# Sliding-window attention's q and k turned by VectorE through DRAM instead of by TensorE

## The chip, the cores and the metric

One core of a Trainium2 chip runs the whole program. The metric is the device time of one execution in microseconds (us); for the kernel before, three executions took 1803.64, 1803.77 and 1804.32, median 1803.77.

## What is computed

Two layers of a decoder trunk over 512 tokens of width 2048, float32 in and out. Per layer: RMS norm, one input projection (2048 x 7192), four mixers of four heads each, side by side, each times a SiLU gate, and one output projection (2048 x 2048) plus the residual. The mixers are called A (gated linear attention, GLA), B (sliding window attention), C (differential attention) and D (gated delta net). B and C matter here:

```
# B: 4 query heads and 2 key heads of 128, window of 128 tokens, tile N of 128 queries sees tiles N-1 and N
q = rms_norm(q.reshape(Bn, N, W, G, R, d), q_g);  k = rms_norm(k.reshape(Bn, N, W, G, d), k_g)
s = jnp.einsum('bgrnid,bgnjd->bgrnij', q, kb) * d ** -0.5
s = jnp.where(valid, s - m_h * dist, -jnp.inf)
mx = jnp.maximum(jnp.max(s, -1), sink); p = exp(s - mx); p = p / (sum(p) + exp(sink - mx))
o = jnp.einsum('bgrnij,bgnjd->bgrnid', p, vb)
# C: 4 heads with two q and two k of 64 each
q = rms_norm(q.reshape(Bn, T, H, 2, dq), q_g) * dq ** -0.5;  k = rms_norm(k.reshape(Bn, T, H, 2, dq), k_g)
w = softmax(s[0]) - lam_full * softmax(s[1]);  o = w @ v
```

## The kernel before

The order of each engine is written out by hand, as five instruction streams with semaphores. `Steps` (line 67) numbers the steps of one stream on one semaphore; `X.one("3.q")` marks the step, `X.at(l, "3.q")` is the value that others wait for. Letters: B_PE, B_ACT, B_DVE are B's steps on TensorE, ScalarE and VectorE, N_ACT and N_DVE those of the norms of B's and C's q and k.

TensorE works through dense products (`project`, line 539): one of 14 chunks of 512 columns of the input projection, 16 steps of the inner dimension (kt) times 4 banks times 3 matmuls, then the output projection. Weights stream in through the SP and POOL queues. Between these dense matmuls `project` opens breaks: it takes `stages` pieces from a generator (`mixer`), spread evenly over half steps of 6 dense matmuls each, starting after `skip` steps. A piece ends at a `yield`. TensorE executes in order, so when a piece waits for an operand, the dense product behind it waits too. Each chunk's four banks (`acc`) are taken out by ScalarE (`take_out`, line 1052), and the next chunk's first matmul in a bank waits for that.

The order of chunks is dq dk dv dz bz az aq av bq bkv cq ck cv cz. GLA's tiles 0 to 3 are spread over bq, bkv, cq and ck. B's tiles 0 and 1 are spread over cv, its tiles 2 and 3 over cz (line 1018, 13 pieces each). C follows during the output projection.

A tile t of B in the kernel before, on TensorE (`swa`, line 772): values of tile t-1 and, in the same break, six transposes of the tile's normed q (4 heads) and k (2 heads) (L796, L798); in the next break the scores (L808); three breaks later the turned weights (L824); two later the next tile's values (L783). The two-digit names in the code (`s0`, `s1`, `pt0`, `pt1`) are two heads each. ScalarE copies the turned q and k out of PSUM with their gains (L1382, L1384), and takes the exponentials (L1397). VectorE adds the slopes (L1988), makes maxima, copies half of the turned weights (L2009, step PT1) and scales the outputs (L2020).

C's q and k are turned already without TensorE: squares on ScalarE (L1344), sums (L1948) and products with the inverse norms (L1961) on VectorE, then VectorE transposes of 32 x 32 blocks (L1975), four DMAs from ScalarE's queue into the DRAM tensor `hops` (L1393) and eight back (`hop_back`, L1364), which put the blocks in their places. All four tiles must be back when C starts, long after. For B and C the norms of tile t+1 are made during tile t: `squares`, `sums`, `inverses` (logarithm and exponential, each with a table load) and `normalise`, q and k of both mixers together.

DMAs that ScalarE issues stand in its instruction order. In the trace they are on ACTq.

## Time and profile before

| | |
|---|---|
| median of three executions | 1803.77 us |
| the profiled execution | 1804.25 us, its span 1802.5 us |
| granted TensorE clock, mean over the span | 1.000 |
| PE busy | 1795.4 us |
| VectorE, ScalarE, GpSimd busy | 917.9, 501.3, 920.8 us |
| local attention of layer 0 (cv and cz) | about 589 to 692 us |

The profile is of one execution. A timeline row gives start, length, engine, line, operation, the written and the read tensor, the shape and the count of merged instructions; in square brackets stands how long the engine was idle before and what it waited for. Matmuls are pipelined, so their lengths overlap; the distance of two starts says more. Lines are those of the kernel before.

### The profile page before, as it was taken

To read this page: it belongs to the slowest core of one execution; us is meant where nothing else is said; L and a number is where in the kernel's file an instruction comes from. 1 tells how busy PE (TensorE), PEld (TensorE's weight loads), DVE (VectorE), ACT (ScalarE), POOL (GpSimd) and SP (SyncE) were. 2 spreads that over 40 slices of the span, in tenths; PEclk is the share of its full clock that TensorE was granted. 3 is DMA by queue.
4 is the path that set the end of the run, shared out by engine and by line. 5 is a ranking of instruction groups with operands and counts; after the bars stand their busy time and mean duration, and the time that the engine had idled before them with its cause. 6 is when DMAs were issued, how large, how long until landed. Compare 5 with 4: busy or idle time off the path is not lost.

```text
span 1802.5 us, 23457 instructions
## 1 busy us (share of the span) xinstructions
PE 1795.4 (100%) x9254; PEld 1478.6 (82%) x9254; DVE 917.9 (51%) x1959; ACT 501.3 (28%) x959; POOL 920.8 (51%) x864
## 2 busy tenths in 40 slices
PE   9999999999999999999999999999999999999999
PEld 7788888888888888788887888888888888887887
DVE  7546825525433675544644478264344337755342
ACT  6212214022222543322312131141222225333220
POOL 6555544545555444445565555445455555444444
PEclk9999999999999999999999999999999999999999
DMA  7566554655555667455775656545555566674556
GB/s 276 166 189 210 168 161 152 183 149 177 182 177 175 207 199 251 140 160 175 253 225 171 188 187 192 159 149 180 158 175 181 165 186 200 201 254 140 164 164 210
DMA packets 108334, 333.39 MB, mean 185 GB/s; under 512 B 11680, under 2 KB 24512, under 8 KB 107968
## 3 DMA queue, kind: packets, MB, share of 16 engines
q1 hardware_dynamic: 43904, 155.73, 27.3%
q0 software_dynamic: 40320, 146.82, 26.8%
q10 hardware_dynamic: 24000, 29.34, 4.8%
q8 instruction: 73, 1.20, 0.3%
q14 instruction: 37, 0.30, 0.1%
HBM read 319.25 MB, written 12.60 MB: 184 GB/s over the span
## 4 chain that ended last, share of the span: by engine, by line
PE 95%; DVE 3%; DMA 1%; ACT 1%; issue 0%; SPq 0%; ACTq 0%
PE acc L563 84%; PE mix L612 2%; PE mix L853 1%; DVE actT_lo L1536 1%; DMA w_raw<-in_wstream 1%; PE mix L783 1%; PE mix L873 1%; PE mix L808 1%; PE mix L606 1%; PE mix L886 1%; DVE slots L2028 0%; PE mix L760 0%; PE mix L982 0%; PE mix L963 0%; DVE slots L1564 0%; DMA slots<-in_x 0%
## 5 line engine op out<-in xcount | busy, mean ns | idle before, releaser
L520 POOL TENSOR_TENSOR w_lo<-w_raw,w_hi 128x512 fp32r<-128x512 f32 x575 | 761.2, 1326 | 616.6 <-DMA w_hi<-in_wstream 462.7
L563 PE MATMUL acc<-w_hi,actT_hi 128*128 128x512 f32 x1408 | 558.8, 397 | 0.0
L563 PE MATMUL acc<-w_hi,actT_lo 128*128 128x512 f32 x1408 | 548.7, 390 | 0.0
L563 PE MATMUL acc<-w_lo,actT_hi 128*128 128x512 f32 x1408 | 548.4, 389 | 0.0
L563 PE MATMUL acc<-actT_hi,w_hi 128*128 128x512 f32 x896 | 357.5, 399 | 0.8 <-issue 0.4
L563 PE MATMUL acc<-actT_hi,w_lo 128*128 128x512 f32 x896 | 349.5, 390 | 0.0
L563 PE MATMUL acc<-actT_lo,w_hi 128*128 128x512 f32 x896 | 349.3, 390 | 0.0
L563 PEld LDWEIGHTS acc<-w_hi,actT_hi 128*128 128x128 f32 x1408 | 264.5, 188 | 55.5 <-issue 2.8
L563 PEld LDWEIGHTS acc<-w_hi,actT_lo 128*128 128x128 f32 x1408 | 264.3, 188 | 55.7
L563 PEld LDWEIGHTS acc<-w_lo,actT_hi 128*128 128x128 f32 x1408 | 264.6, 188 | 51.9
L491 POOL DMA_DIRECT2D w_hi<-in_wstream x280 | 159.2, 569 | 252.6 <-PE acc L563 239.3
L563 PEld LDWEIGHTS acc<-actT_hi,w_hi 128*128 128x128 f32 x896 | 168.3, 188 | 47.1 <-issue 12.8
L563 PEld LDWEIGHTS acc<-actT_hi,w_lo 128*128 128x128 f32 x896 | 168.2, 188 | 35.9
L563 PEld LDWEIGHTS acc<-actT_lo,w_hi 128*128 128x128 f32 x896 | 168.5, 188 | 32.9 <-issue 0.5
L2028 DVE TENSOR_TENSOR slots<-acc,slots 128x512 f32<-128x512 f32 x64 | 42.8, 689 | 84.8 <-PE acc L563 84.8
L1626 DVE SCALAR_TENSOR_TENSOR slots<-slots,pcol_all 128x511 f32<-128x511 f32 (+2 forms) x72 | 84.7, 1181 | 1.7
L1058 ACT ACTIVATE slots<-acc,xr 128x512 f32<-128x512 f32 x56 | 37.8, 690 | 167.9 <-PE acc L563 167.9
L1606 DVE TENSOR_TENSOR slots<-acc,slots 128x512 f32<-128x512 f32 x24 | 15.7, 688 | 125.0 <-PE acc L563 91.8
L1882 DVE SCALAR_TENSOR_TENSOR slots<-mix,slots 128x256 f32<-128x256 f32 x8 | 3.4, 424 | 133.3 <-ACT slots L1301 133.3
L612 PEld LDWEIGHTS mix<-slots 128*128 128x128 f32 x400 | 48.5, 191 | 2.0
L612 PE MATMUL mix<-slots 128*128 128x128 f32 x400 | 49.0, 275 | 0.0
L1874 DVE STREAM_TRANSPOSE slots<-slots 32x512 f32<-32x512 f32 x64 | 45.0, 703 | 1.9
(269 smaller groups left out, 1608.3 us busy)
## 6 DMA issues: line engine op xcount, KB each, us to landing
w_raw<-in_wstream SPq DMA_DIRECT2D x288, 512.0 KB, 4.5
w_hi<-in_wstream POOLq DMA_DIRECT2D x280, 512.0 KB, 3.8
out_x<-slots ACTq DMA_DIRECT2D x7, 1024.0 KB, 8.4
slots<-hops ACTq DMA_DIRECT2D x64, 64.0 KB, 2.7
slots<-in_x ACTq DMA_DIRECT2D x1, 4096.0 KB, 19.4
slots<-out_x ACTq DMA_DIRECT2D x1, 4096.0 KB, 19.9
slots<-in_x SPq DMA_DIRECT2D x3, 1024.0 KB, 12.5
slots<-rows ACTq DMA_DIRECT2D x2, 1024.0 KB, 7.3
```

Of the source, the lines that this page charges most:

```text
L491: pool.dma_start(w_hi[:, g % HI].rearrange("p a n -> p (a n)"), wstream[g:g + 1].rearrange("a p n -> p (a n)")).then_inc(hi_in[g % HI], 16)
L520: pool.tensor_tensor(w_lo[:, n % RING], w_raw[:, g % RAW, k], w_hi[:, g % HI, k].bitcast(F32), ALU.subtract).then_inc(w_ready, 1)
L563: last = nc.tensor.matmul(acc[b][:, :], lhsT, rhs, start=(k == 0 and i == 0), stop=(k == kts - 1 and i == 2))
L606: last = nc.tensor.transpose(mh[i][:, h], s[:, h, t * P:t * P + P], ident)
L612: last = nc.tensor.matmul(mh[bank][:, h], lhsT[:, h], rhs[:, h], start=True, stop=True)
L783: last = nc.tensor.matmul(mh[2][:, h], W["PT"][:, h, P * m:P * m + P], kv[:, t + 1 - n + m, 256 + (h // 2) * HD:256 + (h // 2) * HD + HD], ...
L808: last = nc.tensor.matmul(mix[2 + h // 2][:, 256 * (h % 2):256 * (h % 2) + P * n], W["QT"][:, h], kv[:, t + 1 - n:t + 1, (h // 2) * HD:(h ...
L853: last = nc.tensor.matmul(mix[m][:, 0:P * n], qT[r, t, h], kT[r, 0:n, :, h].rearrange("p t b c -> p (t b) c"), start=True, stop=True)
L1058: nc.scalar.activation(slot(SLOT[c])[:, b], acc[b][:, :], ACT.Copy, scale=r) \
L1626: dve.scalar_tensor_tensor(dst[:, d:], src[:, 0:SEQ - d], tap[i], dst[:, d:], ALU.mult, ALU.add).then_inc(CONV_DVE.sem, CONV_DVE.one(f"{c} ...
L1874: dve.transpose(dst[fs, :, :, rs_], src[rs_, :, :, fs]) \
L2028: dve.tensor_tensor(xs, acc[b][:, :], xs, ALU.add).then_inc(acc_free, 1)
```

## The change

1. B's q and k are turned like C's: VectorE transposes of 32 x 32 blocks in one instruction each (q 512 columns, k 256), two stores per tile into a new DRAM tensor `hops_b`, eight loads back (`b_out`, `b_back`), all from ScalarE's queue. q returns to its slot, is copied with both gains into QT (the gain of k is multiplied into that of q at the start); k returns to its slot and is read there by the scores.
2. TensorE's transposes go. The scores of tile t stand in the break of the values of tile t-1, one break earlier than before; the scores of a pair of tiles are two matmuls of 128 columns per head instead of one of 256. The scores use banks 0 and 1, the turned weights 2 and 3 (it was the other way round).
3. The norms are split in two streams: B's two tiles ahead, C's one tile ahead. B's tiles 0 and 1 are normed within GLA's last tile, and tile 0 is turned and stored there.
4. C's turns are one instruction each for q and k; the source buffers are `general` (which its squares use too), two stores of 256 KB instead of four of 128 KB. C's q comes back into `ws` and is scaled from there into its slot (`scaled_q`), tile by tile.

Core of the diff, old helpers that only move left out:

```diff
-        out += ([f"{t-1}.pv"] if t else []) + [f"{t}.{x}" for x in "tr s0 s1 pt0 pt1".split()]
+        out += ([f"{t-1}.pv"] if t else []) + [f"{t}.{x}" for x in "s0 s1 pt0 pt1".split()]
...
-SWA_ACT = "gate qT kT p0 p1 p2 p3 es PT0".split()
+SWA_ACT = "gate qT p0 p1 p2 p3 es PT0".split()
 SWA_DVE = "b0 b1 b2 b3 mx mxs nm es g3 den rd PT1 y0 y1 y2 y3".split()
-TURNED = "q0 q1 k0 k1".split()
-
-NORM_ACT = "bq bk cq ck lnb lnc rb rc".split()
-NORM_DVE = "redb redc bq bk cq ck".split()
+TURNED = "q k".split()
+
+NORM_B_ACT, NORM_B_DVE = "q k ln r".split(), "red q k".split()
+NORM_C_ACT, NORM_C_DVE = "q k ln r".split(), "red q k".split()
...
-        turned_piece = dict(q0=smT[:, 0:256], q1=smT[:, 256:512], k0=wlr_sb[:, :], k1=s6[:, 768:1024])
+        turned_b = dict(q=smT[:, :], k=wlr_sb[:, :])
+        turned_c = dict(q=general[:, 0], k=general[:, 1])
...
-                pe.wait_ge(N_DVE.sem, N_DVE.at(l, f"{t}.bk"))
-                for h in H:
-                    nc.tensor.transpose(mh[0][:, h], q[:, t, h * HD:h * HD + HD], ident)
-                for g in range(2):
-                    last = nc.tensor.transpose(mh[1][:, g], kv[:, t, g * HD:g * HD + HD], ident)
-                last.then_inc(B_PE.sem, B_PE.one(f"{t}.tr"))
-                yield
-
-                pe.wait_ge(B_ACT.sem, B_ACT.at(l, f"{t}.kT"))
-                if t:
-
-                    pe.wait_ge(B_DVE.sem, B_DVE.at(l, f"{t-1}.y3"))
+                pe.wait_ge(hop_b_k, 64 * (TILES * l + t + 1))
+                pe.wait_ge(B_ACT.sem, B_ACT.at(l, f"{t}.qT"))
                 n = min(t, 1) + 1
                 for h in H:
-                    last = nc.tensor.matmul(mix[2 + h // 2][:, 256 * (h % 2):256 * (h % 2) + P * n], W["QT"][:, h],
-                                            kv[:, t + 1 - n:t + 1, (h // 2) * HD:(h // 2) * HD + HD],
-                                            start=True, stop=True)
+                    for m in range(n):
+                        c = 256 * (h % 2) + P * m
+                        last = nc.tensor.matmul(mix[h // 2][:, c:c + P], W["QT"][:, h], kT[:, t + 1 - n + m, h // 2],
+                                                start=True, stop=True)
                     if h % 2:
...
-                pe.wait_ge(B_ACT.sem, B_ACT.at(l, f"{t}.kT"))
+                if t:
+                    pe.wait_ge(B_DVE.sem, B_DVE.at(l, f"{t-1}.y3"))
                 for i in range(2):
 
                     pe.wait_ge(B_ACT.sem, B_ACT.at(l, f"{t}.p{2*i+1}"))
                     for h in (2 * i, 2 * i + 1):
                         for m in range(n):
-                            last = nc.tensor.transpose(mix[i][:, 256 * (h % 2) + P * m:256 * (h % 2) + P * m + P],
+                            last = nc.tensor.transpose(mix[2 + i][:, 256 * (h % 2) + P * m:256 * (h % 2) + P * m + P],
                                                        W["SB"][:, h, P * m:P * m + P], ident)
                     last.then_inc(B_PE.sem, B_PE.one(f"{t}.pt{i}"))
                 yield
                 yield
+                yield
...
+                def b_out(t):
+
+                    for c, cs in (("q", slice(0, GW)), ("k", slice(GW, GW + 256))):
+                        act.wait_ge(TB_DVE.sem, TB_DVE.at(l, f"{t}.{c}"))
+                        act.dma_start(hops_b[l, :, t, cs], turned_b[c]).then_inc(hop_b_out, 16)
+
+                def b_back(t):
+
+                    act.wait_ge(hop_b_out, 32 * (TILES * l + t + 1))
+                    for to, start, n, landed in ((slot(SLOT["bq"])[:, t], 0, P, hop_b_q),
+                                                 (slot(SLOT["bkv"])[:, t, 0:256], GW, 2 * BLK, hop_b_k)):
+                        for r in range(P // BLK):
+                            act.dma_start(to[BLK * r:BLK * r + BLK].rearrange("p (b c) -> p b c", b=P // BLK),
+                                          hops_b[l, :, t, start + n * r:start + n * r + n]
+                                          .rearrange("(b p) c -> p b c", b=P // BLK)).then_inc(landed, 16)
...
+                    if t == TILES - 1:
+                        act.wait_ge(acc_free, acc_free_after(l, CHUNKS.index("bkv"), 3))
+                        w(A_DVE, "ki")
+                        for i in range(2):
+                            squares_b(i)
+                            inverses(i, None)
...
+                    if t == TILES - 1:
+                        b_out(0)
...
+                def scaled_q(t):
+
+                    act.wait_ge(hop_q, 64 * (TILES * l + t + 1))
+                    nc.scalar.activation(slot(SLOT["cq"])[:, t].rearrange("p (h b c) -> p h b c", h=HEADS, c=BLK),
+                                         ws[:, :].rearrange("p (b h c) -> p h b c", h=HEADS, c=BLK), ACT.Copy,
+                                         scale=pcv(l, PC["gq_c"])).then_inc(Q_ACT.sem, Q_ACT.one(f"q{t}"))
+
+                def c_out(t):
+
+                    for i, c in enumerate("qk"):
+                        act.wait_ge(TC_DVE.sem, TC_DVE.at(l, f"{t}.{c}"))
+                        act.dma_start(hops[l, i, :, t], turned_c[c]).then_inc(hop_out, 16)
+
+                b_back(0)
                 act.wait_ge(acc_free, acc_free_after(l, CHUNKS.index("ck"), 3))
                 act.wait_ge(A_DVE.sem, A_DVE.at(l, f"{TILES-1}.y3"))
-                squares(0)
-                inverses(0)
+                squares_c(0)
+                inverses(None, 0)
                 for t in T:
                     w = lambda st, s, t=t: act.wait_ge(st.sem, st.at(l, f"{t}.{s}"))
                     s = lambda step, t=t: (B_ACT.sem, B_ACT.one(f"{t}.{step}"))
-                    kv = slot(SLOT["bkv"])[:, t]
                     if t:
 
                         act.wait_ge(B_DVE.sem, B_DVE.at(l, f"{t-1}.g3"))
                     nc.scalar.activation(W["GATE"], slot(SLOT["bz"])[:, t].rearrange("p (h c) -> p h c", h=HEADS),
                                          ACT.Tanh).then_inc(*s("gate"))
-                    w(B_PE, "tr")
-                    nc.scalar.activation(W["QT"], mh[0], ACT.Copy, scale=pcv(l, PC["gq_b"])) \
-                        .then_inc(*s("qT"))
-                    nc.scalar.activation(kv[:, 0:256], mix[1][:, 0:256], ACT.Copy,
-                                         scale=pcv(l, PC["gk_b"])).then_inc(*s("kT"))
+                    act.wait_ge(hop_b_q, 64 * (TILES * l + t + 1))
+                    nc.scalar.activation(W["QT"].rearrange("p h (b c) -> p h b c", c=BLK),
+                                         slot(SLOT["bq"])[:, t].rearrange("p (b h c) -> p h b c", h=HEADS, c=BLK),
+                                         ACT.Copy, scale=pcv(l, PC["gq_b"])).then_inc(*s("qT"))
                     if t + 1 < TILES:
-                        squares(t + 1)
+                        b_out(t + 1)
+                    if t:
+                        c_out(t)
+                    if t + 2 < TILES:
+                        squares_b(t + 2)
+                    if t:
+                        scaled_q(t - 1)
+                        act.wait_ge(Q_ACT.sem, Q_ACT.at(l, f"q{t-1}"))
+                        hop_back(t)
+                    if t + 1 < TILES:
+                        b_back(t + 1)
+                        if t:
+                            squares_c(t + 1)
                     n = P * (min(t, 1) + 1)
...
-                    if t:
-                        hop_back(t - 1)
-                    for i, p in enumerate(TURNED):
-                        act.wait_ge(T_DVE.sem, T_DVE.at(l, f"{t}.{p}"))
-                        act.dma_start(hops[l, i // 2, :, t, 256 * (i % 2):256 * (i % 2) + 256], turned_piece[p]) \
-                            .then_inc(hop_out, 16)
                     w(B_DVE, "nm")
...
                     w(B_DVE, "es")
                     nc.scalar.activation(sd, sd, ACT.Exp).then_inc(*s("es"))
+                    if t == 0:
+                        c_out(0)
+                        hop_back(0)
+                        squares_c(1)
+                    if t + 1 < TILES:
+                        inverses(t + 2 if t + 2 < TILES else None, t + 1)
                     w(B_PE, "pt0")
                     nc.scalar.activation(W["PT"][:, 0:2, 0:n],
-                                         mix[0][:, :].rearrange("p (h c) -> p h c", h=2)[:, :, 0:n], ACT.Copy) \
+                                         mix[2][:, :].rearrange("p (h c) -> p h c", h=2)[:, :, 0:n], ACT.Copy) \
                         .then_inc(*s("PT0"))
...
-                    if t + 1 < TILES:
-                        inverses(t + 1)
                     if t == 1:
                         take_out(l, "cv")
-                hop_back(TILES - 1)
...
-                act.wait_ge(hop_in, 128 * TILES * (l + 1))
-                for t in T:
-                    nc.scalar.activation(slot(SLOT["cq"])[:, t], slot(SLOT["cq"])[:, t], ACT.Copy,
-                                         scale=pcv(l, PC["gq_c"])).then_inc(Q_ACT.sem, Q_ACT.one(f"q{t}"))
+                scaled_q(TILES - 1)
...
+                def turn_b(t):
+
+                    if TILES * l + t:
+                        dve.wait_ge(hop_b_out, 32 * (TILES * l + t))
+                    dve.wait_ge(NB_DVE.sem, NB_DVE.at(l, f"{t}.k"))
+                    for c, src, n in (("q", slot(SLOT["bq"])[:, t], HEADS), ("k", slot(SLOT["bkv"])[:, t, 0:256], 2)):
+                        dve.transpose(turned_b[c].rearrange("p (r h c) -> p r h c", h=n, r=P // BLK), in_blocks(src, n)) \
+                            .then_inc(TB_DVE.sem, TB_DVE.one(f"{t}.{c}"))
...
+                        sum_b(0)
+                        norm_b(0)
+                        turn_b(0)
+                        sum_b(1)
+                        norm_b(1)
...
+                turn_b(1)
+                sum_c(0)
...
+                    if t == 0:
+                        norm_c(0)
+                    if t + 2 < TILES:
+                        sum_b(t + 2)
                     if t + 1 < TILES:
-                        sums(t + 1)
+                        sum_c(t + 1)
                     gz = slot(SLOT["bz"])[:, t].rearrange("p (h c) -> p h c", h=HEADS)
                     gate(B_DVE, l, t, gz, W["GATE"])
...
+                    if t + 2 < TILES:
+                        norm_b(t + 2)
+                        turn_b(t + 2)
                     if t + 1 < TILES:
-                        normalise(t + 1)
-                        turn_c(t + 1, TURNED[:2])
+                        norm_c(t + 1)
...
+    args.append(nc.dram_tensor("hops_b", (DEPTH, P, TILES, GW + 256), F32, kind="Internal").ap())
```

## Rows read from the trace of the kernel before

**Rows 1.** The page: engine totals, and the chain that ended last by engine.
```profile
PE 1795.4 (100%) x9254; PEld 1478.6 (82%) x9254; DVE 917.9 (51%) x1959; ACT 501.3 (28%) x959; POOL 920.8 (51%) x864
...
PE 95%; DVE 3%; DMA 1%; ACT 1%; issue 0%; SPq 0%; ACTq 0%
```

**Rows 2.** PE timeline at the first tile: start us, length us, engine, line, operation.
```profile
598.64 0.40 PE L563 MATMUL acc<-w_hi,actT_lo 128*128 128x512 f32 x1
598.87 0.60 PE L796 MATMUL mix<-cf_sb,slots 128*128 128x128 f32 x4
599.31 0.38 PE L798 MATMUL mix<-cf_sb,slots 128*128 128x128 f32 x2
...
599.76 0.39 PE L563 MATMUL acc<-w_lo,actT_hi 128*128 128x512 f32 x1
```

**Rows 3.** PE timeline, later breaks of the same stretch.
```profile
602.28 1.05 PE L808 MATMUL mix<-slots 128*128 128x128 f32 x8
...
617.27 1.05 PE L783 MATMUL mix<-slots 128*128 128x128 f32 x8
...
621.57 1.89 PE L808 MATMUL mix<-slots 128*128 128x256 f32 x8
...
640.52 1.95 PE L783 MATMUL mix<-slots 128*128 128x128 f32 x16
642.30 0.60 PE L796 MATMUL mix<-cf_sb,slots 128*128 128x128 f32 x4
```

**Rows 4.** ACT timeline, end of GLA to tile 1; brackets: idle time before.
```profile
587.50 2.73 ACT L1058 ACTIVATE slots<-acc,xr 128x512 f32<-128x512 f32 x4 [9.34 <-PE acc L563]
...
591.11 1.14 ACT L1344 ACTIVATE general<-slots 128x512 f32<-128x512 f32 x2
...
605.01 0.40 ACT L1397 ACTIVATE slots<-slots,stat 128x128 f32<-128x128 f32 x1 [2.37 <-DVE stat L1996]
...
627.01 0.51 ACT L1397 ACTIVATE slots<-slots,stat 128x256 f32<-128x256 f32 x1 [5.08 <-DVE stat L1996]
```

**Rows 5.** ACT and ACTq timeline after the last tile; ACTq is the DMA queue.
```profile
677.67 4.15 ACTq L1364 DMA_DIRECT2D slots<-hops  x8
682.20 5.02 ACT L1330 ACTIVATE actT_hi<-slots,pcol_all 128x512 fp32r<-128x512 f32 x8 [3.94 <-PE acc L563]
```

**Rows 6.** DVE timeline, tile 0 to tile 1.
```profile
608.62 2.90 DVE L1874 STREAM_TRANSPOSE slots<-slots 32x512 f32<-32x512 f32 x4
...
612.00 0.42 DVE L2009 COPY slots<-mix 128x256 f32<-128x256 f32 x1
615.52 0.69 DVE L1956 TENSOR_TENSOR slots<-slots,stat 128x512 f32<-128x512 f32 x1 [3.10 <-ACT stat L1355]
...
616.47 1.28 DVE L1961 TENSOR_TENSOR slots<-slots,stat 128x512 f32<-128x512 f32 x2
```

**Rows 7.** Groups by line: count, busy us, mean ns.
```profile
L1948 DVE TENSOR_REDUCE stat<-general 128x16 f32<-128x1024 f32 x8 | 9.7, 1212 | 0.2
...
L1811 DVE STREAM_TRANSPOSE slots<-slots 32x256 f32<-32x256 f32 x16 | 7.0, 436 | 0.5
```

**Rows 8.** DMA issues of 590 to 680 us: KB each, median us to landing.
```profile
hops<-smT ACTq DMA_DIRECT2D x8, 128.0 KB, 2.3
...
hops<-slots ACTq DMA_DIRECT2D x4, 128.0 KB, 3.8
```

**Rows 9.** PE's first matmuls in the timeline, and a later group of their shape.
```profile
1.49 4.58 PE L532 MATMUL mix<-smT 128*128 128x256 f32 x10 [1.49 <-DVE smT L1504]
...
L532 PE MATMUL mix<-smT 128*128 128x256 f32 x10 | 4.6, 644 | 1.5 <-DVE smT L1504 1.5
...
L732 PE MATMUL mix<-halves 128*128 128x256 f32 x16 | 3.9, 325 | 0.7 <-DVE halves L1887 0.7
```

**Rows 10.** By line: shortest, median and longest ns, of DMA issues and gates.
```profile
L1364 ACTq DMA_DIRECT2D slots<-hops x64: 325/453/1548, 619.0 to 1578.5; - x64
...
L1573 DVE SCALAR_TENSOR_TENSOR slots<-slots x32: 676/684/2316, 223.5 to 1730.8; 128x512 f32<-128x512 f32 x32
```

141 lines of the change are left out of this document (71 added, 70 removed).

## The prediction

> **What bounds the kernel now.** First the page: TensorE (PE) is busy 1795.4 of 1802.5 us and is 95% of the chain that ended last [rows 1]. So a change pays only by what it takes off PE, and it costs every microsecond that PE has to wait. I therefore read PE's timeline in the stretch of local attention, where the dense product runs at one matmul every 0.23 us (598.64 to 598.87 [rows 2]; 0.227 in the mean over longer runs of them) and is broken open for the mixers' small matmuls. No row there has idle time in brackets: every break finds its operands ready. Then I read ScalarE (ACT), its DMA queue (ACTq) and VectorE (DVE), to see how much earlier the operands are ready; that cover is what the change spends.
>
> **What PE gains.** The first break with transposes: dense matmuls start at 598.64 and 599.76, with one dense matmul of 0.227 between the transposes and the second of them. So six transposes cost 1.12 - 2 x 0.227 = 0.67 us, 0.11 each, and the break itself next to nothing (six times 0.11 is all of it) [rows 2]. The change drops four such groups per layer: 2.7 us. For tiles 1 to 3 the scores become 16 records of 128 columns instead of 8 of 256. The 16 values matmuls of the same shape run from 640.52 to 642.30, 1.78 us; the 8 wide ones take 1.89 by their row, and 1.73 by the dense starts around them [rows 3]. That is even, and so is the closed break: I put both at 0, with bounds of -0.2 and +0.3 a layer. Gain: 2.7 us a layer, 5.4 in all. If nothing else happened, 1803.8 would become 1798.4.
>
> **What moves onto ScalarE's queue.** Per tile the old code issues 4 DMAs out and 8 back. The new one issues 2 + 2 out and 8 + 8 back: 20 instead of 12, 32 more a layer, all in ACT's own order. What is an issue worth? At 677.67 ACTq issues 8 DMAs in 4.15 us, 0.52 each, and the next ACT instruction (L1330, whose operands were ready) starts only at 682.20 [rows 5]. So an issue holds back every ACT instruction behind it. I take 0.50 us each, with bounds 0.45 (the median [rows 10]) and 0.60. The Trainium skill ("DMA: Bandwidth & Descriptors", Anatomy of one DMA) puts the sequencer's dispatch at about 50 ns, though in a table for the other issuing path; by an issue of that price all waits below would vanish and the time would be the 1798.4 of the gain alone. The row above speaks against it. From issue to landing of a store into `hops` takes 2.3 to 3.8 us [rows 8]; the new ones are twice as large, 256 KB. I take 2.6, bounds 2.0 and 3.0.
>
> **GLA's last tile.** The new squares, two logarithm/exponential pairs, norms and one turn stand between GLA's gate and its output scale. By the rows' sizes (a pair with its table loads about 3.1 us, VectorE's wait ahead of 615.52; norm of q and k 0.95, turn 0.72 [rows 6] + 0.44 [rows 7]) GLA's last write comes some 5.5 us later and ACT is free again near 583. Its next duty is to take out `ck` from 587.50, after 9.34 us of idle time before [rows 4]. Cover of 4.5 us is left: cost 0. If it were gone, PE would wait for accumulators.
>
> **The first scores.** `b_back(0)` puts 8 issues (4.0) before the squares of differential attention at about 589.4. Then follow squares 1.14 [rows 4], sum 1.21 [rows 7], the pair, gate and the scaled copy of q: done near 599.0. PE now wants this at 598.87, where the transposes stood [rows 2]. Cost 0.2 a layer, bounds 0 and 1.
>
> **Stall A, values of tile 0.** VectorE's sums for tile 1 now wait for `squares_c(1)`, which stands in ACT's order behind `c_out(0)` and `hop_back(0)`; behind the sums are queued the gate, the blocks of `az` and the copy of the turned weights (PT1) for which PE waits. The chain: scores at 598.87; maxima 2.7 later (602.28 to 605.01 now [rows 3, 4]) = 601.6; norm and turn of C's q and k 1.28 + 2 x 0.72 [rows 6] = 604.3; landing 2.6 = 606.9; 8 issues 4.0 = 610.9; squares 1.14 and sum 1.21 = 613.3; gate 0.7 (the median; one took 2.3 [rows 10]), blocks 2.90, two small ones 0.4, PT1 0.42 [rows 6] = 617.7. PE's values stand at 617.27 now; without the transposes they come at 616.6. Stall 1.1 us. In the old order PT1 was at 612.00, since the squares needed no DMA.
>
> **Stall B, turned weights of tile 1.** Both sides count from the end of that PT1 copy. PE: values 0.89, scores 1.76, then six half steps of the dense product (36 x 0.227 = 8.2) until it asks for the exponentials: 10.8. The other side: norm of B's tile 2, 0.95 to 1.1, its turn 1.1, norm and turn of C's tile 1, 2.7, so 4.8; landing 2.6 = 7.5; `hop_back(1)` and `b_back(2)`, 16 issues, 8.0 = 15.5; `squares_c(2)` 1.14 = 16.7; two exponentials of 0.51 [rows 4] = 17.7. The exponentials were ready to start long before: their wait on VectorE ends 5.4 after the scores start, and ACT idles 5.08 before them now [rows 4]. Stall 6.9 us, and 0.6 more since the second pair of exponentials takes longer than the first pair's transposes.
>
> **Stall C, turned weights of tile 2.** ACT waits in its order for the last bank of `cv`, so it counts from the start of the `cz` product: four issues out 1.9 with a landing, together 4.1; 16 issues 8.0 = 12.1; squares 1.14 and two exponentials 1.0 = 14.3. PE: one half step 1.4, values and scores 3.56, six half steps 8.2 = 13.1. Stall 1.2, and 0.6 for the second pair. Tile 3 has nothing to bring back for B behind it: 0.
>
> **PE's clock.** Nowhere in this trace does PE sit idle for longer than 1.5 us, and its granted clock is full. Its first matmuls, after it had done nothing, take 4.58 us for ten records, 0.46 each; the same shape later takes 0.325 by its own duration against 0.644 there [rows 9]: the 1.2 GHz level at the start. A wait of 6.9 us is unlike anything shown. Once a layer it may bring that level back. Bounds: 0, and half of such a stretch, 2.3 us. No row lies between, so I take the middle, 1.2. The Trainium skill ("TensorE: Matmul & The Clock Gate", Part 1) says that the clock falls to half after idling and comes back after sustained work; by that rule the upper bound would hold, 2 us more over both layers. No stretch here can show it.
>
> **The sum.** Per layer: -2.7 + 0.2 + 1.1 + 7.5 + 1.8 + 1.2 = +9.1. Both layers have the same order, so +18.2. The profiled execution has a span of 1802.5 and took 1804.25; against it 1822.4 to the tenth. The median is 1803.77, 0.5 lower, so 1822.0. Issues come in uneven lengths (0.33 to 1.55 [rows 10]), so I round to 1822.
>
> **The rivals.** *R0, the forecast*: PE stalls as worked out, two parts large. With issues of 0.45, landings of 2.0 and no clock loss it is +4.2 a layer, 1812; with 0.60, 3.0 and the full clock loss +16.9 a layer, 1837. *R1, faster*: the issues do not hold ACT back, or the hardware takes them faster when nothing else is in the queue; then the exponentials start with VectorE as now and only the 2.7 us a layer remain: 1798.4. It decides from about 0.2 us an issue: stall B is then 4.8 + 2.6 + 3.2 + 2.2 - 10.8 = 2.0, and with its 0.6 it just eats the gain. For it speaks only that PE never waits today; against it the 4.15 us of idle ACT [rows 5]. *R2, about even*: the stalls are there but half as long, 1802 to 1807, if most DMAs are taken at the shortest durations. *R3, worse at the start*: GLA's extra work outlasts its 4.5 us of cover and the accumulators are taken out late; from then on each microsecond late is a microsecond of PE in each layer, 2 to 6 us on top: 1826 to 1834. It needs VectorE's two-operand instructions at their long durations (0.68 median, 2.3 at most for L1573 [rows 10]); inside the range. *R4, it does not do what it says*: the transposes go, the waits and DMAs are in the code, so only the closed break could be nothing, 0.3 us.
>
> **How the numbers follow.** R0 with R3 0.80, R1 0.12, R2 0.08. What a measurement of this kernel can tell from no change is about 0.2%, 3.6 us. The range leaves out R1 and the upper tail of R0 (0.05): from 1801 to 1836. Faster 0.12, same 0.08, slower 0.80.
>
> **What the profile after would show.** The transposes L796 and L798 gone; per layer three idle times of PE: about 1 us ahead of the values of tile 0, about 7 ahead of the turned weights of tile 1 with the releaser ACT (its exponentials), about 1 to 2 ahead of those of tile 2. ACTq shows 16 issues in a row of about 8 us ahead of the exponentials, and PE's dense matmuls after the long wait perhaps at double distance. Wrong it would be if exponentials run during the issues, if the issues take 0.2 us, or if `squares_c` turns out not to wait for the landing.

## The result, and the profile of the changed kernel

The changed kernel takes 1843.17 us (median of 4 runs, 1841.94 to 1844.06) against 1804.05 us for the kernel before on the same chip: ratio 1.021, 95% interval 1.0198 to 1.0222. It is slower, as forecast, but by 39.1 us and not by 18.2; the time lies 7 us above the range. The profiled execution took 1844.06 us with a span of 1842.3. On another chip the same kernel took 1841.21 us against 1805.59 (four runs, 1837.50 to 1846.65).

The page first (lines of the engines' totals and of the chain; for [rows 1]):

```profile
PE 1802.3 (98%) x9254; PEld 1478.8 (80%) x9254; DVE 935.6 (51%) x1927; ACT 509.0 (28%) x959; POOL 920.7 (50%) x864
...
PE 89%; DMA 3%; ACTq 3%; DVE 2%; ACT 2%; issue 0%; SPq 0%; DVEq 0%
```

TensorE's share of the chain fell from 95% to 89%; ScalarE's queue and DMAs took its place. Where it waits is in its timeline (start, length, engine, line; idle time and releaser in brackets). In [rows 2, 3] no line has brackets.

```profile
606.00 1.13 PE L807 MATMUL mix<-slots 128*128 128x128 f32 x8 [1.71 <-ACT slots L1422]
...
623.59 0.39 PE L569 MATMUL acc<-w_hi,actT_lo 128*128 128x512 f32 x1
629.58 2.05 PE L790 MATMUL mix<-slots 128*128 128x128 f32 x8 [5.61 <-DVE slots L2071]
631.42 3.42 PE L807 MATMUL mix<-slots 128*128 128x128 f32 x16
634.60 0.48 PE L569 MATMUL acc<-w_hi,actT_hi 128*128 128x512 f32 x1
...
647.40 0.63 PE L823 MATMUL mix<-cf_sb,slots 128*128 128x128 f32 x4 [4.34 <-ACT slots L1442]
648.29 1.12 PE L823 MATMUL mix<-cf_sb,slots 128*128 128x128 f32 x4 [0.26 <-ACT slots L1442]
...
677.96 2.01 PE L823 MATMUL mix<-cf_sb,slots 128*128 128x128 f32 x8 [4.76 <-ACT slots L1442]
```

These are the first scores, the values of tile 0, and the turned weights of tiles 1 and 2. The transposes L796 and L798 are gone. Note the lengths behind the waits: 16 scores matmuls take 3.42 us where 16 of the same shape took 1.95 in [rows 3]. The windows say why (length, PE, PEld, DVE, ACT and POOL busy with counts, PEclk, DMA share, GB/s):

```profile
623.60:629.50 5.90, 0.37 (x2) 0.00 (x0) 5.25 (x10) 5.23 (x10) 1.67 (x2) 0.85 0.60 178
629.50:634.60 5.10, 5.02 (x24) 5.05 (x25) 5.00 (x12) 0.29 (x1) 0.00 (x0) 0.51 0.31 110
634.60:642.70 8.10, 8.10 (x39) 6.66 (x37) 4.99 (x11) 1.26 (x3) 3.04 (x3) 1.00 0.70 218
647.30:652.50 5.20, 4.84 (x18) 3.97 (x19) 5.01 (x10) 4.89 (x12) 0.48 (x1) 0.67 0.25 84
677.30:682.00 4.70, 4.04 (x14) 3.39 (x15) 4.51 (x9) 4.64 (x13) 0.00 (x0) 0.50 0.04 9
```

Behind each of the three long waits the mean granted clock of the window is 0.50 to 0.67, that is mostly the 1.2 GHz level, and in the one window that lies later (634.60) it is 1.00 again.

ScalarE and its queue over tiles 0 to 2 (for [rows 4, 5]):

```profile
609.02 3.90 ACTq L1332 DMA_DIRECT2D slots<-hops_b  x8
612.97 0.40 ACT L1442 ACTIVATE slots<-slots,stat 128x128 f32<-128x128 f32 x1 [6.29 <-issue]
613.22 0.34 ACTq L1406 DMA_DIRECT2D hops<-general  x1
...
613.61 0.44 ACTq L1406 DMA_DIRECT2D hops<-general  x1
...
618.88 2.04 ACTq L1391 DMA_DIRECT2D ws<-hops  x4
620.96 1.90 ACTq L1391 DMA_DIRECT2D slots<-hops  x4
622.90 1.15 ACT L1305 ACTIVATE general<-slots 128x512 f32<-128x512 f32 x2 [8.19 <-issue]
...
633.35 0.92 ACTq L1406 DMA_DIRECT2D hops<-general  x2
...
636.65 1.78 ACTq L1391 DMA_DIRECT2D ws<-hops  x4
638.46 2.28 ACTq L1391 DMA_DIRECT2D slots<-hops  x4
640.78 4.30 ACTq L1332 DMA_DIRECT2D slots<-hops_b  x8
645.12 1.15 ACT L1305 ACTIVATE general<-slots 128x512 f32<-128x512 f32 x2 [9.26 <-issue]
646.18 0.49 ACT L1442 ACTIVATE slots<-slots,stat 128x256 f32<-128x256 f32 x1
```

The exponentials L1442 and the squares L1305 start when the issues in front of them have ended. VectorE waits for those squares, and behind them stands the copy L2071 for which TensorE waits (for [rows 6]):

```profile
608.89 2.38 DVE L1958 TENSOR_TENSOR slots<-slots,stat 128x512 f32<-128x512 f32 x2
611.20 1.29 DVE L1962 STREAM_TRANSPOSE general<-slots 128x512 f32<-128x512 f32 x2
...
624.09 1.22 DVE L1951 TENSOR_REDUCE stat<-general 128x16 f32<-128x1024 f32 x1 [10.77 <-ACT general L1305]
...
629.04 0.39 DVE L2071 COPY slots<-mix 128x256 f32<-128x256 f32 x1
```

To see what every stage costs, I took the start of the n-th matmul of the dense product (there are 6912, in the same order in every kernel) and subtracted its start in the kernel before. The table has this difference in us at six points: ahead of and behind local attention and behind differential attention, in both layers (the end is behind differential attention of layer 1). The kernels other than the changed one are those of the experiments below.

| kernel | ahead of local, layer 0 | behind it | behind differential | ahead of local, layer 1 | behind it | end |
|---|---|---|---|---|---|---|
| changed | +5.3 | +26.6 | +23.7 | +23.7 | +41.6 | +39.2 |
| changed, again | -0.7 | +19.5 | +16.4 | +16.8 | +36.3 | +33.9 |
| one load of four | +0.2 | +2.9 | +0.9 | +1.2 | +6.8 | +4.4 |
| c's loads from SyncE | -1.0 | +4.3 | +1.2 | +4.1 | +4.2 | +2.0 |
| exponentials first | +1.2 | +8.4 | +5.3 | +5.5 | +12.6 | +10.2 |
| all loads from SyncE | +2.2 | +0.9 | -1.6 | -1.4 | -1.9 | -4.4 |
| both mends | +0.5 | -1.8 | -5.0 | -4.9 | -7.3 | -8.1 |
| kernel before, q of C sorted | +1.4 | +1.4 | -1.6 | +0.1 | +0.1 | -2.3 |
| changed, q of C as before | +1.6 | +24.2 | +23.6 | +23.7 | +43.1 | +43.0 |

So local attention costs 17.9 to 21.3 us a layer, and differential attention gives back 2.4 to 3.1, which the forecast did not have. Stages without any part of the change wander by 1 to 5 us from one execution to the next, so the first execution's 39.2 are 33.9 us of the changed stages and 5.3 from its start; in the repeat the end stands 34.6 above the point ahead of local attention. The other three executions of the first series took 1841.9 to 1843.5 us and have no profile, so what they lost at the start isn't known.

### The profile page after: what moved, and what is told of

Same layout as the page of the kernel before. It is cut to its first block, busy times and chain, and to the rows that moved or that the text cites. A ratio compares the mean times of both kernels' runs of the same rounds, so it can differ in the third digit from the quotient of the medians.

```text
span 1842.3 us, 23474 instructions
## 1 busy us (share of the span) xinstructions
PE 1802.3 (98%) x9254; PEld 1478.8 (80%) x9254; DVE 935.6 (51%) x1927; ACT 509.0 (28%) x959; POOL 920.7 (50%) x864
## 4 chain that ended last, share of the span: by engine, by line
PE 89%; DMA 3%; ACTq 3%; DVE 2%; ACT 2%; issue 0%; SPq 0%; DVEq 0%
PE acc L569 78%; PE mix L618 2%; ACTq L1332 2%; DMA hops<-general 1%; ACTq L1391 1%; PE mix L853 1%; DMA w_raw<-in_wstream 1%; PE mix L873 1%; PE mix L612 1%; ACT slots L1058 1%; DMA hops_b<-wlr_sb 1%; ACT general L1305 1%; PE mix L823 0%; DMA slots<-in_x 0%; PE mix L766 0%
```

## The experiments

**Does ScalarE's order hang on the issues or on the landings?** Two kernels take work out of the queue and leave out that part of the result. The first:

```diff
 # b_back and hop_back
-                        for r in range(P // BLK):
+                        for r in range(1):
 # and the waits on what they load
-                pe.wait_ge(hop_b_k, 64 * (TILES * l + t + 1))
+                pe.wait_ge(hop_b_k, 16 * (TILES * l + t + 1))
```

> The changed kernel with only one of the four loads of each group of four (4 issues per tile on ScalarE's queue instead of 16; three quarters of the turned q and k don't come back, which is the part of the computation that is left out). Stores, order and waits stay. Theory A, the issue time of the loads sets ScalarE's order: the 8 + 8 issues ahead of tile 1's exponentials (7.2 to 8.4 us at about 0.45 to 0.5 each) become 4 (2 us), the 4.3 us and 4.8 us waits of TensorE before the turned weights of tiles 1 and 2 go, the 7.6 us wait before tile 0's values shrinks by 12 issues (5.4 us), and with the clock loss behind the long waits (about 1.3 us each) some 17 us a layer come back: about 1810 us (1806 to 1818). Theory B, the landings of the stores set it (5.3 to 6.1 us measured against 2.6 in the forecast): the waits shrink by a few us at most, over 1828 us.

Measured: 1808.94 us against 1804.81, ratio 1.003 (1.002 to 1.004); 4.1 us over the kernel before are left of 39.1. The waits before turned weights went in layer 0 (3.7 us stayed in layer 1); before tile 0's values 2.9 us stayed (1.2 in layer 1):

```profile
604.92 0.94 ACTq L1406 DMA_DIRECT2D hops<-general  x2
610.73 0.33 ACTq L1391 DMA_DIRECT2D ws<-hops  x1
...
619.87 1.13 PE L790 MATMUL mix<-slots 128*128 128x128 f32 x8 [2.89 <-DVE slots L2071]
```

What stayed is a landing: the loads of c's tile 0 start 5.8 us after the stores' issue. The second kernel also stores only a quarter of the columns (of b's stores likewise, not shown):

```diff
-                        act.dma_start(hops[l, i, :, t], turned_c[c]).then_inc(hop_out, 16)
+                        act.dma_start(hops[l, i, :, t, 0:P], turned_c[c][:, 0:P]).then_inc(hop_out, 16)
```

> The kernel with one load of four, and with only a quarter of the columns of every store into DRAM (64 KB and 32 KB instead of 256 and 128; the same part is left out as before, no more of it is read). Theory A, issues: as the run before it within 3 us, since the stores are as many. Theory B, landing by size: the stores' landing falls from 4.6 us (median) to about 2.5 us and the wait before tile 0's values loses another 2 to 4 us a layer: 4 to 8 us below the run before it. Third possibility, landing is queueing behind the streams of the weights whatever the size: medians stay at 4 us or more and the time stays.

Measured: 1801.12 us, ratio 0.9981 (0.9971 to 0.9991), 7.8 us below the first. The stores of c land in 3.2 us (median) instead of 4.5, and the wait before tile 0's values is gone (2.8 us of waits before turned weights came in its place in each layer). So both count: the first kernel gave 34 us of the 42, the second the rest. That the 34 are the issues is not shown by these two alone, since fewer bytes move as well; the kernels that issue all loads elsewhere show it further down.

**Is it the size of a store, or what else is moving?** c's stores cut in two of 128 KB, the size that [rows 8] are of:

```diff
-                        act.dma_start(hops[l, i, :, t], turned_c[c]).then_inc(hop_out, 16)
+                        for half in (slice(0, 256), slice(256, 512)):
+                            act.dma_start(hops[l, i, :, t, half], turned_c[c][:, half]).then_inc(hop_out, 16)
```

> The changed kernel with c's stores into DRAM as four of 128 KB a tile, as before, instead of two of 256 KB; all else stays. Theory of size: a 128 KB store lands 2.6 us after its issue as the forecast took it from the kernel before, so the waits ahead of the loads shrink by 2 us or more per tile: 1832 to 1837 us. Theory of load: in the changed kernel a store landed in 2.8 us where the DMA engines were at 0.45 and moved 164 GB/s, and in 5.3 and 6.1 us where they were at 1.08 and 0.94 and moved 294 and 297 GB/s, so cutting it changes nothing, and two more issues cost 0.4 to 0.5 us each: 1841 to 1846 us.

Measured: 1847.83 us against 1804.59, ratio 1.0239 (1.0222 to 1.0256), 43.2 us over the kernel before where the changed kernel had 39.1, and 2 us more than the theory of load gave. One store of 128 KB now takes 3.0 us in the median and 7.2 at most, but ScalarE waits for the last of four. Smaller stores bought nothing here, with the same sum of bytes. What goes with the landing time is in these windows of the changed kernel, each from the issue of c's stores to the loads (columns as above):

```profile
613.20:618.80 5.60, 5.60 (x28) 4.65 (x27) 0.12 (x1) 1.52 (x9) 3.10 (x3) 1.00 1.08 294
633.40:636.60 3.20, 3.20 (x17) 2.85 (x17) 3.17 (x10) 1.55 (x3) 0.06 (x1) 0.83 0.45 164
661.00:667.50 6.50, 6.50 (x46) 5.96 (x45) 4.19 (x10) 1.63 (x3) 2.18 (x2) 1.00 0.94 297
```

Landings of 5.3 and 6.1 us fell where the DMA engines were full, with weights and the small packets of the other hop; 2.8 us where they were half idle. All sixteen of c's stores in this trace go the same way: the four with a DMA share under 0.5 in their first 3 us landed in 2.3 to 2.6 us, the twelve with 0.8 or more in 3.3 to 6.0. It isn't the whole of it, and no run varies the load alone: in the kernel before, eleven of the 32 stores of 128 KB took 3.8 to 5.7 us and the others 2.0 to 2.7, at shares of 0.5 to 0.9 for both. The cause of slow landings stays open.

**Is it the issuing as such, or where it stands in ScalarE's order?** The same instructions in another order (VectorE's `sum_c(t + 1)` moves behind its copy of the turned weights as well):

```diff
                         squares_b(t + 2)
-                    if t:
-                        scaled_q(t - 1)
-                        act.wait_ge(Q_ACT.sem, Q_ACT.at(l, f"q{t-1}"))
-                        hop_back(t)
-                    if t + 1 < TILES:
-                        b_back(t + 1)
-                        if t:
-                            squares_c(t + 1)
                     w(B_DVE, "nm")
...
                     nc.scalar.activation(sd, sd, ACT.Exp).then_inc(*s("es"))
                     if t == 0:
                         c_out(0)
-                        hop_back(0)
-                        squares_c(1)
+                    if t + 1 < TILES:
+                        b_back(t + 1)
+                    if t:
+                        scaled_q(t - 1)
+                        act.wait_ge(Q_ACT.sem, Q_ACT.at(l, f"q{t-1}"))
+                    hop_back(t)
+                    if t + 1 < TILES:
+                        squares_c(t + 1)
```

> The changed kernel with the same instructions, only ordered otherwise: on ScalarE the exponentials of a tile stand ahead of both groups of 8 loads and of the squares of c's next tile, on VectorE the sum of c's squares stands behind the copy of the turned weights. Theory of order: nothing of the issues (16 x 0.45 us) or of the landings (4.6 us) stands ahead of the exponentials any more; TensorE waits about 1 us before tile 0's values, 0.4 before scores and turned weights of tile 1, about 2 us where the next projection waits for its banks: +1.6 to +2.5 us a layer in local attention with the transposes' -2.7 counted, -2.8 a layer in the differential scores, +5.2 at the start if that belongs to the changed kernel: about 1808 us (1803 to 1815). Rival, it is not the order but load on the DMA engines and the clock: over 1830 us.

Measured: 1814.74 us, ratio 1.0053 (1.0038 to 1.0068). The order gives 29 us of the 39, at the upper edge of what was expected. No wait before turned weights is left, but the copy for the values (ScalarE's PT0) now stands behind the issues: 4.1 and 5.0 us of waits before values. Sixteen issues have to stand ahead of something. (Before the first scores 1.8 us are left in layer 0, and ahead of the dense product 1.0 and 0.6 us for a bank that `take_out` frees late.)

**Or on another engine.** SyncE issues all loads, put between its streams of weights (number of the weight load: hop and tile); ScalarE only waits for c's stores ahead of the squares that overwrite them:

```diff
+HOPS_AT = {99: [("b", 0)], 101: [("b", 1)], 102: [("c", 0)], 104: [("b", 2), ("c", 1)],
+           107: [("b", 3), ("c", 2)], 110: [("c", 3)]}
...
                         weights(l * PAIRS + i)
+                    for load, t in HOPS_AT.get(i, ()):
+                        (b_back if load == "b" else hop_back)(l, t)
```

> The changed kernel in its own order, but with all loads of the two hops issued by SyncE, put between its streams of weights; stores stay on ScalarE, and ScalarE waits for c's stores to land only where it overwrites what they read (ahead of the squares). Theory A, ScalarE is held by 16 issues a tile: TensorE's waits all but go, at most 1.5 us a layer are left: about 1801 us (1797 to 1808) with +5.2 at the start, -2.7 and -2.8 a layer. Theory B, it is held by landings: the waits before tile 0's values stay at 3 us or more: over 1812 us. Rival, SyncE's waits hold the weights back: TensorE waits for w_lo, over 1815 us.

Measured: 1798.84 us, ratio 0.9966 (0.9954 to 0.9979): faster than before. The same 64 loads a layer, at nearly the same length per issue (median 0.43 us against 0.45), cost next to nothing on a queue behind which nothing urgent stands. The bytes and the stores are the same as in the changed kernel, so what went, 45 us, is where the loads are issued. Two waits of 0.9 and 1.3 us are left, before tile 0's values. With only c's eight loads a tile moved:

```diff
+HOPS_AT = {102: 0, 104: 1, 107: 2, 110: 3}
...
+                    if i in HOPS_AT:
+                        hop_back(l, HOPS_AT[i])
```

> The changed kernel with only c's 8 loads a tile issued by SyncE; the local attention's 8 stay on ScalarE ahead of the exponentials. If ScalarE's time is a plain sum of issues, half of them away takes 3.9 us from the wait before tile 0's values (7.6 to 3.7) and 3.6 to 4 us from each wait before turned weights (4.3 to 4.8 us to under 1), with their clock loss: 25 to 30 us of the 42 us that moving all 16 gave, 1814 us (1809 to 1819). If it is one group alone, the local attention's, that counts: over 1830 us. If it is c's alone: 1801 us or less.

Measured: 1805.59 us, ratio 1.0006 (0.9996 to 1.0017). By the differences to the kernel before (39.1 us, now 1.0, and -6.0 with all loads moved) half of the issues gave 38 of 45 us, and not the 60 to 70% that were expected. It is no plain sum; the reading, argued from the waits that are left, is that once the issues are shorter than the cover the rest of them is free. Then both mends, the loads on SyncE and the order on ScalarE and VectorE:

```diff
                     if t == 0:
                         c_out(0)
-                        hop_back(0)
-                        squares_c(1)
+                    if t:
+                        scaled_q(t - 1)
+                    if t + 1 < TILES:
+                        act.wait_ge(hop_out, 32 * (TILES * l + t + 1))
+                        squares_c(t + 1)
...
```

> Both mends at once: loads issued by SyncE and the exponentials ahead of the wait for c's stores. The kernel with loads from SyncE alone took 1798.8 us and had two waits of 0.9 and 1.3 us left before tile 0's values. If order is still worth something these two go: 1796.5 us (1795 to 1798). Rival: the waits that are left are covered by the next landing anyway, or scaling and squares now stand ahead of the copy of the turned weights (in the kernel with the order alone that copy was late by 3.7 us before values): 1799 to 1803 us.

Measured: 1795.53 us against 1805.59, ratio 0.9945 (0.9932 to 0.9957), the fastest of all. TensorE has no wait in local attention, in either layer. Local attention gives 2.3 and 2.4 us there: what the change takes off TensorE in this stage is worth 4.7 us of 1805, once nothing waits. SyncE's issues and the break that cost 10.9 us in the changed kernel (values of tile 0 and scores of tile 1, against the dense product at full speed) and costs 2.7 here:

```profile
611.04 1.94 SPq L474 DMA_DIRECT2D ws<-hops  x4
613.03 1.85 SPq L474 DMA_DIRECT2D slots<-hops  x4
...
617.15 1.05 PE L820 MATMUL mix<-slots 128*128 128x128 f32 x8
618.04 1.95 PE L837 MATMUL mix<-slots 128*128 128x128 f32 x16
```

**The gain that the forecast missed.** In differential attention q was written back so that a head's columns stood four apart, and the change writes them side by side. In the kernel before with this part alone (ScalarE's scaling, which has to read all of q anyway, also sorts it, into other buffers) and in the changed kernel with this part undone (the line that reads q; the copy that writes it changes with it, not shown):

```diff
 # the first, in the kernel before
-                qT = slot(SLOT["cq"]).rearrange("p t (c h) -> p t h c", h=HEADS)
+                qT = {i: scaled_to(i).rearrange("p (h c) -> p h c", h=HEADS) for i in T}[t]
 # the second, in the changed kernel
-                qT = slot(SLOT["cq"]).rearrange("p t (h c) -> p t h c", h=HEADS)
+                qT = slot(SLOT["cq"]).rearrange("p t (c h) -> p t h c", h=HEADS)
```

> The kernel before, with only one part of the change: the differential attention's q is written back as contiguous blocks of heads, the scaling also sorts it, and so the weights of its score products are loaded from consecutive columns instead of every fourth. Theory of stride: the loads of weights fall from 316 to 321 ns to about 185 ns, the products from 649 and 432 ns to 588 and 350 ns, 2.5 to 3.1 us a layer: 1798.5 us (1797.5 to 1800), faster than before. Rival, the gain of the changed kernel in that stage came from elsewhere (its scaling done tile by tile earlier): the time stays within 1.5 us of before.

> The changed kernel with only that one part undone: q of the differential attention is sorted to every fourth column, as before. Theory of stride: 2.5 to 3.1 us a layer are lost, the loads of weights take 316 ns again: 1848.8 us (1847 to 1851). Rival: 1843 us, no change.

Measured: 1800.18 us, ratio 0.9971 (0.996 to 0.9983), for the first, 5.4 us faster than before; 1847.41 us, ratio 1.0232 (1.0216 to 1.0248), for the second, 6.2 us over the changed kernel on the same chip (4.2 over its first median, on another). The first came out 0.2 us above the range that was expected for it, the second inside. By the table differential attention gives 3.0 and 2.4 us in the first kernel and 0.6 and 0.1 in the second. The groups of layer 0's differential attention in the kernel before, in the changed one and in the first experiment (matmuls, and loads of weights, PEld):

```profile
L853 PE MATMUL mix<-slots 64*128 64x512 f32 (+1 forms) x32 | 9.2, 649 | 0.0
L886 PE MATMUL mix<-slots 64*128 64x256 f32 (+1 forms) x32 | 5.0, 432 | 0.0
L853 PEld LDWEIGHTS mix<-slots 64*128 64x128 f32 x32 | 4.4, 316 | 1.9 <-issue 0.7 <-DVE slots L2094 0.4 <-DVE stat L2098 0.4
```

```profile
L853 PE MATMUL mix<-slots 64*128 64x512 f32 (+1 forms) x32 | 8.2, 588 | 0.0
L886 PE MATMUL mix<-slots 64*128 64x256 f32 (+1 forms) x32 | 3.7, 350 | 0.0
L853 PEld LDWEIGHTS mix<-slots 64*128 64x128 f32 x32 | 2.4, 185 | 1.9 <-issue 1.1 <-DVE slots L2158 0.4
```

```profile
L856 PEld LDWEIGHTS mix<-slots,general 64*128 64x128 f32 x32 | 2.4, 184 | 1.9 <-issue 1.1 <-DVE slots L2101 0.4
```

A load of weights from every fourth column takes 316 ns and from neighbouring ones 185 ns, 2.3 us in layer 0 in the products' own time. Both experiments agree.

**The 5.2 us at the start.** In the first profile the work was late before local attention had begun. The changed kernel again:

> The changed kernel itself, once more, for its profile: in the first one the work was 5.2 us late by the 16th k tile already, before the change has any instruction of its own but one sum of constants. If that belongs to the kernel, it comes again (5 us late at the first layer's projections) and local attention and what follows cost 34 us over both layers. If it was that execution's, the start agrees with before within 1.5 us, and either the time is nearer 1838 us or the waits of local attention are longer by as much.

Measured: 1841.21 us, ratio 1.02 (1.0181 to 1.0219), and -0.8 us at the same place. It was that execution's, as were the 2 to 3 us by which other profiles are late there. In the first profile a wait of 1.53 us ahead of the projection's small matmuls (L948) was followed by a low clock, where most of the 5.2 us were lost:

```profile
51.00:56.50 5.50, 5.50 (x14) 3.79 (x14) 0.08 (x1) 2.85 (x5) 1.26 (x1) 0.50 0.33 96
```

Three other kernels with a wait as long at the same place (1.53 or 1.54 us) kept their full clock. Local attention costs 20.2 and 19.5 us in the repeat.

**The clock.** Into the kernel with both mends, which has no wait in local attention, goes a delay that is neither a DMA nor a landing, in `squares_b` of tile 3, which ScalarE runs ahead of tile 1's exponentials:

```diff
+                    for i in range(12 if t == TILES - 1 else 0):   # 8 in the second kernel
+                        nc.scalar.activation(W["SQ"][:, 0:4].rearrange("p g c -> p (g c)"), slot(SLOT["bq"])[:, t],
+                                             ACT.Square).then_inc(again, 1)
+                        act.wait_ge(again, 12 * l + i + 1)
```

> The kernel with both mends (1795.5 us, no wait of TensorE left in local attention), and ahead of tile 1's exponentials ScalarE squares the same tile of q 12 times more, each time waiting for the last: about 0.65 us each, 7.8 in all, less the 2.0 us that ScalarE idles there and the 1.3 us that the exponentials are early. TensorE then waits some 4.5 + 0.6 us before tile 1's turned weights, once a layer, with no DMA and no landing as its cause. Theory of idling: the wait alone brings the granted clock down, as the waits of 4.3 to 5.6 us did in the changed kernel, where each break cost 2.0 to 2.7 us over its wait and its work: 7.2 us a layer, 1810 us (1807 to 1813). Rival: the clock fell there for another reason (load of the DMA engines, power of all engines together): only the wait is paid, 1805.5 us (1804 to 1806.5).

> As the run before it with 8 squares more instead of 12: the wait is about 1.9 + 0.6 us. Waits of 0.9 to 1.7 us have cost nothing beyond themselves so far, and waits of 2.9 and 3.7 us 2.0 us more. If a wait of about 2 us is still free of a clock loss: 1800.5 us (1799 to 1802). If it already costs one: 1804.5 us (1803 to 1806).

Measured: 1806.98 us against 1805.45, ratio 1.0009 (0.9999 to 1.0018), for twelve; 1798.61, ratio 0.996 (0.9947 to 0.9972), for eight. The first lies between what the two theories gave, the second under both, because the waits came out shorter than meant (3.3 and 3.2 us; 2.1 and 1.0). So the times decide nothing by themselves. Read by stage, the first kernel's local attention is 5.2 and 5.1 us slower than without the delay, 6.5 of these 10.3 being the waits. The profile has the rest:

```profile
631.76 0.63 PE L854 MATMUL mix<-cf_sb,slots 128*128 128x128 f32 x4 [3.00 <-ACT slots L1448]
632.65 1.12 PE L854 MATMUL mix<-cf_sb,slots 128*128 128x128 f32 x4 [0.27 <-ACT slots L1448]
633.42 0.78 PE L600 MATMUL acc<-w_hi,actT_hi 128*128 128x512 f32 x1
633.99 0.63 PE L600 MATMUL acc<-w_lo,actT_hi 128*128 128x512 f32 x1
```

and its clock (windows, columns as above):

```profile
632.00:636.20 4.20, 3.93 (x15) 3.15 (x14) 4.01 (x9) 3.93 (x10) 0.00 (x0) 0.59 0.25 74
636.20:640.00 3.80, 3.80 (x19) 3.13 (x18) 1.91 (x3) 2.39 (x5) 1.97 (x3) 1.00 0.73 205
```

The break cost 6.15 us over the dense product, of which 0.90 is its work and 3.27 its wait: 1.98 more, in dense matmuls 0.43 apart instead of 0.23. So the clock falls behind a wait that no DMA or landing causes, with the DMA engines at 0.25. The same sum for fourteen waits of seven kernels; the costs beyond the wait fall in two groups:

| wait, us | 0.36 | 0.85 | 1.02 | 1.40 | 1.71 | 2.05 | 2.81 | 2.89 | 3.27 | 3.67 | 3.72 | 4.60 | 4.76 | 5.61 |
|---|---|---|---|---|---|---|---|---|---|---|---|---|---|---|
| beyond it, us | 0.2 | 0.2 | 0.4 | 0.2 | 0.2 | 2.0 | 0.4 | 1.9 | 2.0 | 2.9 | 1.9 | 2.0 | 2.3 | 2.6 |

The length of the wait doesn't sort them by itself. The 2.81 us are in layer 1 of the kernel with quarter stores, before turned weights, and its clock stayed full; in layer 0 of the same kernel 2.83 us before the same matmuls cost 1.9 more:

```profile
1528.70 0.63 PE L823 MATMUL mix<-cf_sb,slots 128*128 128x128 f32 x4 [2.54 <-ACT slots L1442]
1529.59 0.66 PE L823 MATMUL mix<-cf_sb,slots 128*128 128x128 f32 x4 [0.27 <-ACT slots L1442]
```

```profile
1525.80:1535.00 9.20, 6.39 (x32) 4.98 (x31) 8.87 (x15) 7.07 (x18) 2.94 (x4) 1.00 0.46 136
633.00:637.00 4.00, 3.81 (x15) 3.01 (x14) 3.81 (x8) 3.94 (x10) 0.00 (x0) 0.57 0.40 131
```

Over all waits in local attention in these profiles: 17 of up to 1.9 us cost 0.2 to 0.4 beyond themselves, 31 of 2.9 us and more cost 1.6 to 3.2, and of the three between (2.05, 2.81, 2.83) two lost the clock. What decides in between is not shown. The eight-square kernel has one wait of each kind (2.05 in layer 0, 1.02 in layer 1). Its runs spread from 1795.8 to 1808.4, more than one clock loss explains (the profiled one, the slowest, was 5.0 us late before local attention), so its median says little. The Trainium skill's rule ("TensorE: Matmul & The Clock Gate", Part 1) that idling sends the clock to its lower level agrees with the rows of the long waits.

## Why the prediction was right in kind and wrong in size

The sum per layer as forecast, and as the profile of the changed kernel has it in layer 0 and layer 1. The waits are the bracketed times, the clock is what the breaks cost beyond wait and undisturbed work (2.73 for values with scores, 0.90 for turned weights, as in the kernel with both mends).

| term | forecast | layer 0 | layer 1 |
|---|---|---|---|
| transposes | -2.7 | -2.7 | -2.7 |
| first scores | +0.2 | +1.7 | +0.4 |
| stall A, values of tile 0 | +1.1 | +5.6 | +5.2 |
| stall B, turned weights of tile 1 | +7.5 | +4.6 | +4.7 |
| stall C, turned weights of tile 2 | +1.8 | +4.8 | +4.4 |
| clock | +1.2 | +7.1 | +5.5 |
| sum | +9.1 | +21.1 | +17.5 |
| differential attention | 0 | -2.9 | -2.4 |

The sums agree with the differences in the table further up (21.3 and 17.9). They leave out the 5.3 us of the first execution's start: with these stages alone it would have been at about 1838 us, still over the range. The transposes' gain is taken from [rows 2]; with both mends local attention came out 2.3 and 2.4 us faster, so it is about right, and the closed break costs a few tenths at most.

*What held.* The mechanism: three stalls a layer at the places named, with the releasers named. The price of an issue: 3.90 to 4.30 us for eight in the rows above (up to 5.5 elsewhere in local attention) against the 4.0 assumed, and they do hold ScalarE back. The 50 ns that the Trainium skill ("DMA: Bandwidth & Descriptors", Anatomy of one DMA) has in its table for the other issuing path were not the price here: the shortest of these issues took 0.31 us, the median 0.45. GLA's last tile: its output came 5.4 us later, within its cover. Moving issues off ScalarE made the kernel faster than before, so rival R1's condition was the right one, only that it wasn't met.

*The clock was the largest error*, 5.9 and 4.3 us a layer. The prediction put the loss between 0 and 2.3 us, took the middle and counted it once. Its upper bound was about right for one wait (1.6 to 2.6 in the changed kernel, up to 3.2 in its repeat), by some luck: it was worked out from the durations of the first ten matmuls [rows 9], for which no row shows a level: the profile's clock records begin at 5.9 us, when they end. But there are three waits a layer that are long enough, and each pays. The step that failed is "once a layer it may bring that level back": stalls A and C had been sized too small to count.

*Stall A, off by 4.5 us*, for three reasons. The chain had c's stores issued 5.4 us after the scores' start, as soon as VectorE had turned q and k. VectorE was done at 612.49, 6.5 us after 606.00: its two products with the norms took 2.38 us, where [rows 6] have 1.28 (in the kernel with one load of four too, so the issues are not the cause, which stays open). Then, in ScalarE's order, the stores stand behind `b_back(1)` and the exponentials, of which the first starts at 612.97, and went out at 613.22 and 613.61, 7.2 and 7.6 us after the scores (5.9 and 6.4 in the kernel with one load of four). And the landing was put at 2.6 us with an upper bound of 3.0, although [rows 8] have a median of 3.8 for a third of the stores they list; the last store landed 5.3 us after its issue. The estimate that follows from the line of the Trainium skill for the other issuing path ("DMA: Bandwidth & Descriptors", Anatomy of one DMA, 2.0 us and the bytes at 436 GB/s) is 2.6 us for 256 KB as well. The measured median of c's stores in the changed kernel is 4.6, so neither was a bound.

*Stall C, off by 3.0 us*, is the landing again: 6.1 us from the second issue to the loads, where issues and landing together had 4.1. *Stall B came out 2.9 us smaller.* The chain's own length was right, 16.75 us from the copy's end to the first exponential against 16.7, but TensorE spent 2.4 us more on values and scores at the lower clock and so asked later. A stall ahead, with the slow clock behind it, is cover for the next one, so waits worked out each at full speed don't simply add up.

*First scores, off by 1.5 us in layer 0*: the eight issues of `b_back(0)` took 5.5 us there (4.15 in layer 1, where the wait is 0.4).

*The missed term.* The prediction priced differential attention at nothing although the diff changes the pattern in which its weights are read. One look at PEld's groups of the kernel before would have shown 316 and 321 ns beside the 140 to 191 ns of the others.

The range failed for the clock and the landings: its upper end had landings of 3.0 us and one clock loss a layer.

## What to carry over

A DMA issue of 0.45 us is not small when eight or sixteen stand ahead of an operation that the busiest engine waits for; read which engine's order they enter, and put them on the queue of an engine with slack (here 45 us for the same transfers). Add to each forecast wait of TensorE that is as long as those here (2 to 6 us) another 2 us for its clock, each by itself (the 31 waits of 2.9 us and more here paid 1.6 to 3.2, of the shorter ones few did), and take the upper bound of a landing from the slowest stores in the trace and not from the median of a calm group. Look at weight loads whose columns are strided: sorting them in a copy that has to be made anyway gave 0.3% on its own.

## What the runs showed that was not expected

Loads of fp32 weights cost 316 ns with a column stride of four and 185 ns without. The Trainium skill ("SBUF — State Buffer", Door 1: The DMA port swizzle) says in a note that consecutive accesses within one line of 16 bytes run at full bandwidth and that crossing to a new line each time pays a penalty; four fp32 columns are 16 bytes, and these numbers fit that, though no run tried another stride. A wait of 2.05 us cost TensorE 2.0 us beyond itself and one of 2.81 us only 0.4. SyncE issues the same loads at 0.43 us in the median (3.65 to 5.4 us for eight) and had room for all 64 a layer: in the kernel with both mends TensorE waited once for weights, 1.2 us, in differential attention of layer 1, which is why that stage gives only 0.8 us there.
